# Local attention heads beside the token products, and the first units of w_out_2 by halves of the tokens between the other heads

## The reference, cut to what matters

```
def second_block(x, positions, norm_g, w_in, swa_sink, ..., w_out, final_norm):
    for l in range(DEPTH_2):
        h = rmsnorm_2(x, norm_g[l])
        proj = jnp.einsum('bsd,de->bse', h, w_in[l])
        (a_q, a_k, a_v, a_g, b_cq, b_ckv, b_kr, b_g,
         c_q, c_k, c_v, c_g) = jnp.split(proj, SPLIT_OFFSETS, axis=-1)
        ya = swa_attention(...)     # 8 local heads of 128, 2 key heads, a sink
        yb = mla_attention(...)     # 4 heads, queries, keys and values from latents
        yc = diff_attention(...)    # 4 pairs of heads of 64, then a norm
        y = jnp.concatenate([ya * jax.nn.silu(a_g), yb * jax.nn.silu(b_g),
                             yc * jax.nn.silu(c_g)], axis=-1)
        x = x + jnp.einsum('bse,ed->bsd', y, w_out[l])
    return rmsnorm_2(x, final_norm)
```

## Time and profile before

| | |
|---|---|
| median of 3 runs | 2373.35 us |
| span of the profiled execution | 2372.3 us |
| TensorE busy | 2273.5 us, 96% |
| VectorE busy | 1363.0 us, 57% |
| ScalarE busy | 1055.6 us, 44% |
| mean granted TensorE clock | 0.978 |

### The profile page before, as it was taken

How to read it: one execution, slowest core, us unless ns; L and a number is a source line. 1 busy time by engine, 2 the same in 40 slices (tenths; PEclk the granted TensorE clock), 3 DMA queues, 4 the chain that set the end, 5 groups by cost and what they waited for, 6 DMA issues and landing times.

```text
span 2372.3 us, 31751 instructions
## 1 busy us (share of the span) xinstructions
PE 2273.5 (96%) x13038; PEld 1973.5 (83%) x13038; DVE 1363.0 (57%) x1694; ACT 1055.6 (44%) x1366; POOL 57.7 (2%) x66
## 2 busy tenths in 40 slices
PE   8999989899989999999999999999998999999898
PEld 7888978787877888888888887888976889898676
DVE  5545656475566666766766444644456454444654
ACT  5433443423455545454555333533445443343543
POOL 0000020011000000000000000000000000000000
PEclk9999998899999999999999999999999999999999
DMA  8556520013634555555565556555531556564033
GB/s 282 193 168 221 178 88 1 1 32 139 202 127 137 190 183 193 179 193 183 189 205 187 194 195 197 195 185 183 170 99 36 178 176 221 162 202 161 1 125 141
DMA packets 235977, 373.07 MB, mean 157 GB/s; under 512 B 8359, under 2 KB 108244, under 8 KB 235092
## 3 DMA queue, kind: packets, MB, share of 16 engines
q1 hardware_dynamic: 229740, 362.89, 46.3%
q10 hardware_dynamic: 6120, 8.50, 1.0%
HBM read 369.25 MB, written 2.12 MB: 157 GB/s over the span
## 4 chain that ended last, share of the span: by engine, by line
PE 64%; DVE 5%; issue 5%; ACT 2%; POOL 0%; DVEq 0%; POOLq 0%; ACTq 0%
PE PS L465 16%; PE PS L424 12%; PE PS L426 12%; PE PS L425 12%; PE PS L468 8%; PE PS L1941 1%; PE PS L1925 1%; DVE w_lo L342 1%; ACT w_hi L337 1%; DVE small L1979 1%; DVE spare L1975 1%; PE PS L904 1%; ACT spare L1953 0%; DVE h_both L921 0%; PE PS L2608 0%
## 5 line engine op out<-in xcount | busy, mean ns | idle before, releaser
L342 DVE TENSOR_TENSOR w_lo<-raw,w_hi 128x2048 fp32r<-128x2048 f32 (+2 forms) x340 | 766.4, 2254 | 766.5 <-ACT w_hi L337 766.2
L337 ACT ACTIVATE w_hi<-raw 128x2048 fp32r<-128x2048 f32 (+2 forms) x340 | 641.2, 1886 | 842.4 <-PE PS L426 487.4
L465 PE MATMUL PS<-h_both,w_hi 128*128 128x512 f32 x1968 | 539.4, 395 | 2.9 <-DVE h_both L921 1.8
L424 PE MATMUL PS<-w_hi,h_both 128*128 128x512 f32 (+2 forms) x1344 | 511.6, 381 | 11.3 <-DVE h_both L921 4.6
L425 PE MATMUL PS<-w_lo,h_both 128*128 128x512 f32 (+2 forms) x1344 | 508.3, 378 | 0.0
L426 PE MATMUL PS<-w_hi,h_both 128*128 128x512 f32 (+2 forms) x1088 | 408.7, 376 | 0.0
L465 PEld LDWEIGHTS PS<-h_both,w_hi 128*128 128x128 f32 x1968 | 336.6, 189 | 49.5 <-DVE h_both L921 2.8
L468 PEld LDWEIGHTS PS<-h_both,w_lo 128*128 128x128 f32 x1968 | 302.1, 189 | 42.1
L468 PE MATMUL PS<-h_both,w_lo 128*128 128x256 f32 x1968 | 313.1, 281 | 0.0
L424 PEld LDWEIGHTS PS<-w_hi,h_both 128*128 128x128 f32 x1344 | 255.3, 190 | 59.8 <-DVE h_both L921 5.1
L425 PEld LDWEIGHTS PS<-w_lo,h_both 128*128 128x128 f32 x1344 | 255.1, 190 | 45.8
(11 more groups left out here) (508 smaller groups left out, 2027.1 us busy)
## 6 DMA issues: line engine op xcount, KB each, us to landing
raw<-in_w_in SPq DMA_DIRECT2D x132, 1024.0 KB, 5.2
raw<-in_ffn_w_up SPq DMA_DIRECT2D x176, 512.0 KB, 4.4
raw<-in_w_out SPq DMA_DIRECT2D x48, 1024.0 KB, 5.1
raw<-in_ffn_w_down SPq DMA_DIRECT2D x44, 1024.0 KB, 5.1
raw<-in_mem_wkv SPq DMA_DIRECT2D x8, 1024.0 KB, 11.6
raw<-in_mem_wq SPq DMA_DIRECT2D x4, 1024.0 KB, 5.3
raw<-in_mem_wo SPq DMA_DIRECT2D x4, 1024.0 KB, 7.0
raw<-in_w_in SPq DMA_DIRECT2D x4, 768.0 KB, 4.7
```

The costliest lines, as they stand in the source:

```text
L337: act.activation(w_hi[:, slot % 2, :st.n], raw[:, slot, :st.n], ACT.Copy).then_inc(hi_made, 1)
L342: dve.tensor_tensor(w_lo[:, slot % 2, :st.n], raw[:, slot, :st.n], w_hi[:, slot % 2, :st.n].bitcast(F32), ALU.subtract).then_inc(lo_made, 1)
L424: pe.matmul(ps, l_hi, r_hi, start=start, stop=False, skip_group_check=skip)
L465: pe.matmul(sums, wh[:, k, cs], h_both[:, :, kk, :], start=kk == 0, stop=False, skip_group_check=True)
```

## The change

- The eight local heads leave the head stage. They run on four lanes of their own (banks 4 to 7) as `fill` between the units of tok and tok_end, one step after each unit, with more rounds between a head's steps. Their lane n starts n + 1 units in. The Silus of their gates move with them (`local_gates_scalar`).
- The head stage keeps 8 diff heads on four lanes (two rounds), the latents and 4 MLA heads (the latter idle for 9 to 11 rounds).
- Their working room moves from `spare` (where the slots of `w_hi` and `w_lo` lie) to other places, so that one of the two split slots can be filled during the stage. The diff heads' squares go to the lane's own room, with one wait on ScalarE for it.
- Unit 0 of w_out_2 is split before the last evacuation of c_vg. Units 0, 1 and 2 are each multiplied in two halves, first the upper 128 tokens, then the lower (`multiply_rows`), at set rounds between the heads. Turns 0 to 3 (the local heads' rows) use bank 7. Unit 3 stays whole.
- The waits at the start of the stage (latents, gates, small loads) stay; semaphores that nothing used are left out.

```
+        def multiply_rows(pe, q, j, t, ready=None):
+            st, bank, slot = q.st, 2 * q.parity + t, (q.first + j) % 2
+            if j == 0 and t == 0:
+                pe.wait_ge(act_evac, q.number(-1))
+                pe.wait_ge(dve_evac, q.number(-1))
+            pe.wait_ge(lo_made, q.unit(j + 1))
+            if ready:
+                ready()
...
+            for k in range(st.kb):
+                kk = j * st.kb + k
+                last = three_pass(pe, PS[:, bank, :st.n_cols], h_hi[:, kk, t * P:(t + 1) * P], h_lo[:, kk, t * P:(t + 1) * P],
+                                  wh[:, k, :], wl[:, k, :], kk == 0, kk == st.units * st.kb - 1)
+            if t == TB - 1:
+                last.then_inc(unit_used, 1)
...
+                if job["h"] == 1:
+                    turns = t_mixed[job["layer"]]
+                    pe.wait_ge(turns.dve, turns["lo3"])
+                elif job["h"] > 1:
+                    diff_made(pe, job["layer"])
...
+        def local_tensor(pe, j):
...
+            (q, k), = job["pairs"]
+            for t_ in range(TB):
+                last = pe.matmul(PS[:, bank, t_ * S:(t_ + 1) * S], q[:, t_ * P:(t_ + 1) * P], k, start=True, stop=True)
+            last.then_inc(j.pe, 1)
+            yield
+            yield
+            yield
+            pe.wait_ge(j.act, j["exp1"])
...
+            last.then_inc(j.pe, 1)
+            yield
+            yield
+            pe.wait_ge(j.act, j["copied"])
...
+            last.then_inc(j.pe, 1)
+            yield
+            yield
...
+        def beside_products(part, e, layer):
+
+            made = L2[layer]["local"]
+            return together(*[one_by_one([rounds(n + 1)] + [part(e, j) for j in js]) for n, js in enumerate(made)])
...
+        def local_gates_scalar(act, layer):
+            g, st = L2[layer]["gates"], ST2[layer]["tok"]
+            for n in range(2):
+                yield from rounds(6 if n == 0 else 4)
+                act.wait_ge(act_evac, st.G + n + 1)
+                act.wait_ge(dve_evac, st.G + n + 1)
+                g_ = ztok[:, :, AG + 512 * n:AG + 512 * (n + 1)]
+                act.activation(g_, g_, ACT.Silu).then_inc(g.act, 1)
...
-            jobs = [latents] + swa + diff + mla
-            for job in jobs:
+            jobs = [latents] + diff + mla
+            for job in swa + jobs:
                 job["layer"] = layer
-            for job in mla[1:]:
-                job["idle"] = 3
-            L2[layer].update(latents=latents, swa=swa, diff_heads=diff)
-            SWA, DIFF_, MLA = 1, 9, 17
-            picks = [[SWA + 6, DIFF_ + 0, DIFF_ + 4], [SWA + 7, DIFF_ + 1, DIFF_ + 5], [0, MLA], [SWA, SWA + 1, MLA + 1],
-                     [DIFF_ + 2, DIFF_ + 6], [DIFF_ + 3, DIFF_ + 7], [SWA + 2, SWA + 3, MLA + 2],
-                     [SWA + 4, SWA + 5, MLA + 3]]
-            return on_lanes(jobs, picks, starts)
+            for job, idle in zip(mla[1:], (9, 11, 11)):
+                job["idle"] = idle
+            L2[layer].update(latents=latents, diff_heads=diff,
+                             local=on_lanes(swa, [[n, 4 + n] for n in range(4)], local_starts, local_lanes))
+            DIFF_, MLA = 1, 9
+            for n in (2, 3):
+                diff[n]["idle"] = 1
+            picks = [[DIFF_ + n, DIFF_ + 4 + n] for n in range(4)] + [[0, MLA], [MLA + 1], [MLA + 2], [MLA + 3]]
+            return on_lanes(jobs, picks, starts, late_lanes)
...
-        MIXED_ROUND = 15
+        MIXED_BANKS = (7, 7, 7, 7, 4, 5, 6, 5)
...
         def mixed_tensor(pe, layer, j):
-            for _ in range(MIXED_ROUND):
-                yield
-            free_lanes_made(pe, layer)
-            for n in (0, 1):
+            q, d = Group(ST2[layer]["out"], 0), L2[layer]["diff"]
+            yield
+            local_made(pe, layer)
+            for n in range(4):
                 mixed_turn(pe, j, n)
-            yield
-            yield
-            for n in (2, 3):
+                if n == 2:
+                    multiply_rows(pe, q, 0, 0, ready=lambda: pe.wait_ge(j.dve, j["lo1"]))
+                yield
+                if n == 2:
+                    multiply_rows(pe, q, 0, 1)
+                yield
+            multiply_rows(pe, q, 1, 0, ready=lambda: pe.wait_ge(j.dve, j["lo3"]))
+            yield
+            yield
+            yield
+            multiply_rows(pe, q, 1, 1)
+            yield
+            pe.wait_ge(d.dve, d["n11"])
+            for n in (4, 5):
                 mixed_turn(pe, j, n)
             yield
+            yield
+            for made in lanes2[layer][4:6]:
+                pe.wait_ge(made[-1].dve, made[-1].dve1)
+            mixed_turn(pe, j, 6)
+            multiply_rows(pe, q, 2, 0, ready=lambda: pe.wait_ge(j.dve, j["lo5"]))
+            yield
 
         def mixed_scalar(act, layer, j):
-            for _ in range(MIXED_ROUND):
-                yield
-            free_lanes_made(act, layer)
-            split_hi(act, Group(ST2[layer]["out"], 0), 0)
-            yield
-            for n in (0, 1):
+            q = Group(ST2[layer]["out"], 0)
+            yield
+            yield
+            for n in range(4):
                 mixed_hi(act, j, n)
-            yield
-            for n in (2, 3):
+                yield
+                if n == 0:
+                    split_hi(act, q, 1)
+                if n == 3:
+                    split_hi(act, q, 2)
+                yield
+            yield from rounds(4)
+            for n in (4, 5):
                 mixed_hi(act, j, n)
+            split_hi(act, q, 3)
+            yield
+            yield
+            mixed_hi(act, j, 6)
             yield
 
         def mixed_vector(dve, layer, j):
-            for _ in range(MIXED_ROUND):
-                yield
-            ssq, d = L2[layer]["ssq"], L2[layer]["diff"]
+            q, ssq, d = Group(ST2[layer]["out"], 0), L2[layer]["ssq"], L2[layer]["diff"]
+            yield
+            yield
+            for n in range(4):
+                mixed_lo(dve, j, n)
+                yield
+                if n == 0:
+                    split_lo(dve, q, 1)
+                if n == 3:
+                    split_lo(dve, q, 2)
+                yield
+            yield
             for job in L2[layer]["diff_heads"]:
                 dve.wait_ge(job["steps"].act, job["steps"].act1)
             dve.tensor_scalar(ssq, ssq, 1.0 / P, EPS, ALU.mult, ALU.add).then_inc(d.dve, 1)
             yield
-            split_lo(dve, Group(ST2[layer]["out"], 0), 0)
-            yield
-            for n in (0, 1):
-                mixed_lo(dve, j, n)
-            yield
-            for n in (2, 3):
-                mixed_lo(dve, j, n)
-            yield
-
-        def mixed_opening_tensor(pe, layer, j):
-            st, d = ST2[layer]["out"], L2[layer]["diff"]
-            multiply(pe, Group(st, 0), 0, ready=lambda: pe.wait_ge(j.dve, j["lo1"]))
-            yield
-            lanes_made(pe, lanes2[layer])
-            pe.wait_ge(d.dve, d["n11"])
-            for n in (4, 5):
-                mixed_turn(pe, j, n)
-            multiply(pe, Group(st, 0), 1, ready=lambda: pe.wait_ge(j.dve, j["lo3"]))
-            yield
-            for n in (6, 7):
-                mixed_turn(pe, j, n)
-            multiply(pe, Group(st, 0), 2, ready=lambda: pe.wait_ge(j.dve, j["lo5"]))
-            yield
-            multiply(pe, Group(st, 0), 3, ready=lambda: pe.wait_ge(j.dve, j["lo7"]))
-            yield
-
-        def mixed_opening_scalar(act, layer, j):
-            q = Group(ST2[layer]["out"], 0)
-            lanes_made(act, lanes2[layer])
-            split_hi(act, q, 1)
-            yield
-            for n in (4, 5):
-                mixed_hi(act, j, n)
-            yield
-            split_hi(act, q, 2)
-            for n in (6, 7):
-                mixed_hi(act, j, n)
-            yield
-            split_hi(act, q, 3)
-            yield
-
-        def mixed_opening_vector(dve, layer, j):
-            q = Group(ST2[layer]["out"], 0)
-            lanes_made(dve, lanes2[layer])
-            split_lo(dve, q, 1)
             run(diff_rows(dve, layer))
+            yield
             yield
             for n in (4, 5):
                 mixed_lo(dve, j, n)
-            yield
-            split_lo(dve, q, 2)
-            for n in (6, 7):
-                mixed_lo(dve, j, n)
-            yield
             split_lo(dve, q, 3)
+            yield
+            yield
+            mixed_lo(dve, j, 6)
+            yield
+
+        def mixed_opening_tensor(pe, layer, j):
+            q = Group(ST2[layer]["out"], 0)
+            lanes_made(pe, lanes2[layer])
+            mixed_turn(pe, j, 7)
+            multiply_rows(pe, q, 2, 1)
+            multiply(pe, q, 3, ready=lambda: pe.wait_ge(j.dve, j["lo7"]))
+            yield
...
-                for name in ("kv", "tok", "tok_end"):
-                    run(products_tensor(pe, st[name]))
+                run(products_tensor(pe, st["kv"]))
+                fill = beside_products(local_tensor, pe, layer)
```

(9 more changed lines are left out.)

190 lines of the change are left out of this document (131 added, 59 removed).

## The result

| | before | after |
|---|---|---|
| median of 4 runs | 2373.36 us (2368.74 to 2374.34) | 2356.7 us (2356.39 to 2357.76) |
| span of the profiled execution | 2372.3 us | 2354.7 us |
| mean granted TensorE clock | 0.978 | 0.982 |

The ratio is 0.9937, 95% interval 0.9923 to 0.9951: the change saves 16.7 us by the medians and 17.6 by the two profiled executions. The forecast was 2356.4, the range 2346 to 2367.

What follows compares the result with a forecast made beforehand. TensorE, busy 96% of the span, loses time only by waiting or running slowly. Per layer 68.0 work, 7.7 waits, 1.7 clock, 18.2 local heads, 1.0 interruptions: 96.6; gains 8.1 and 8.8, together 16.9, give 2356.4 us (2346 to 2367).

Steps and rivals of the forecast that it cites:

- Local heads among the token products: Token products: the heads' 18.2 us per layer move, interruptions add 0.06 each, 1.0 in all; other engines priced at nothing.
- The round with a Silu: ScalarE's densest round in the token products: result ready after 11.6 us, TensorE comes after about 13.9, 2.3 us left.
- Unit 0 split early: Before the last token evacuation: both engines split while TensorE multiplies the last unit, 5.5 us against 1.9 + 2.3; nothing late.
- (a): Start of the stage: TensorE waits 0.9 us for the last evacuation, as before.
- (b): Fifth diff score: TensorE waits 3.0 us for lane 0's puts, behind a VectorE split, then 0.4 for lane 1.
- (c): Seventh diff score: TensorE waits 1.4 us for lane 2's puts, behind a v copy, biases and maxima, then 0.4.
- (d): Last mixed turn: TensorE waits 1.6 us, as VectorE's split of unit 3 stands before the last two puts.
- One half-clock stretch of 1.7 per layer: After the 3 us wait for lane 0's puts: 1.7 us lost once per layer; bounds none and twice 1.7.
- The sum of 96.6: Per layer, token-product end to fourth w_out_2 unit plus moved local heads and interruptions: 96.6 us after, against 104.7 and 105.4.
- Rival 1: Stage waits mostly covered, no half clock follows, interruptions free: 25 us gained in all, 2348; chance 0.2.
- Rival 2: VectorE bounds the short stage: diff-score waits double, second half-clock stretch, about 1.6 us gained per layer, 2370; chance 0.12.
- Rivals 3 and 4: Token products: interruptions dear, at 1.0 us each 2386, chance 0.04; local heads don't fit, splits late, 2387, chance 0.01.

Runs made afterwards that it cites:

- after_again: The changed kernel unmodified, run again as the reference beside three follow-up kernels: median 2350.76 us (2349.37 to 2356.36, 5 runs).
- whole_units: Against the changed kernel, units 0 to 2 of w_out_2 multiplied whole after the last turn, splits of 2 and 3 behind the heads: 2374.85 us.
- late_unit0: Against the changed kernel, both engines split unit 0 of w_out_2 in the stage, right before unit 1: 2363.36 us (2359.54 to 2364.16, 5 runs).

## Why the prediction was right, point by point

- **TensorE's waits in the stage are the lever, its work is not.** Right. TensorE's work is the same (its instructions are the same in number), and 16.2 of the 17.6 us stand between the first matmul of kv and the fourth w_out_2 unit of the two layers. The token products grew by 18.2 where the text had 19.
- **Local heads among the token products: 18.2 moved, 1.0 for 16 interruptions, none of it late.** Measured 18.2 together, so the 1.0 was too much. The interruption was 0.06 in the text and is 0.02 or less by the experiment, and by the rows of one unit less than nothing. The other engines had the room: there is no wait of TensorE in the token products but the 1.8 us one behind them that both kernels have. What the text left out is that the clock can fall behind that wait: in the profiled execution of before it did so in layer 1 alone, in that of after in both, 1.5 us.
- **The round with a Silu has 2.3 us left.** Right by its outcome: the table load is 1283 ns, as in the earlier trace rows, in all five places of the stretch, and no wait follows a Silu. By the Trainium skill's 2.7 us for every change of table set (ScalarE: Activation LUTs, Rules for kernel authors) each of these rounds would have been 0.5 us late; the trace disagrees with that figure. From the end of a split (1613.85) to the start of the Silu behind its table load (1615.17) are 1.32 us.

```profile
L2086 ACT ACT_TABLE_LOAD x3 | 3.8, 1283 | 0.1
...
L2505 ACT ACT_TABLE_LOAD x2 | 2.6, 1283 | 0.0
```

- **Unit 0 split early: nothing is late.** Right, and shown by its reverse. From c_qk to the stage, where the split was added, the stretch without half clock takes 94.37 us before and 94.39 in after_again.
- **(a) 0.9.** As before, 0.89.
- **(b) 3.0 and 0.4.** Measured 2.71 and 1.0. The chain was right in each link, and everything came some tenths later than put. In us from the start of the stage, and each step on VectorE taken as over when the next one starts, the split on ScalarE was put at 14.9 to 16.8 and ran from 15.2 to 17.1, VectorE's split was to end at 19.1 and ended at 19.4, the v copy 19.7 and 20.1, the low part 20.4 and 20.7, the puts 21.0 and 21.2. TensorE was put there at 18.0 and came at 18.6. These are the rows of VectorE:

```profile
1786.36 2.29 DVE L343 TENSOR_TENSOR w_lo<-raw,w_hi 128x2048 fp32r<-128x2048 f32 x1 [3.17 <-ACT w_hi L338]
...
1788.71 0.67 DVE L2777 COPY arena<-PS 128x512 f32<-128x512 f32 x1
1789.30 0.68 DVE L2833 TENSOR_TENSOR h_both<-PS,h_both 128x512 fp32r<-128x512 f32 x1
1789.89 0.60 DVE L2664 TENSOR_SCALAR arena<-PS,small 128x128 f32<-128x128 f32 x2
```

What the walk did not see is that the chain has a second arm of nearly the same length, TensorE's own v product, copy and low part. It makes no difference to the sum, and all of it to what an improvement brings.
- **(c) 1.4 and 0.4.** Measured 1.13 and 0.9.
- **(d) 1.6.** Measured 1.20, and caused by the split, as said.
- **One half-clock stretch of 1.7 per layer.** Right as a mean, not as a rule: behind the same 2.71 us wait the kernel after lost 0 in layer 0 and 1.7 in layer 1, and 3.4 and 1.7 in the other profiled execution.
- **The sum of 96.6.** Measured 77.15 + 18.2 = 95.35 and 78.8 + 18.2 = 97.0. Several misses cancel in it. The visible waits are 5.9 and the pauses of the two second lanes 1.9, together 7.8, where the text had 7.7. TensorE's own work is 77.15 - 7.8 = 69.3 in layer 0 and not 68.0: it is put together in smaller pieces, a half unit takes 12 matmuls of 0.227 and about 0.1 more, and each wait has the tail of a group before it. Against these 1.3 stand the 1.0 for interruptions, which cost nothing, and in layer 0 the 1.7 of half clock that did not come: 96.6 + 0.1 + 1.3 - 1.0 - 1.7 = 95.3. In layer 1 it came.
- **The stage of 77 to 78 us.** Measured 77.15 and 78.8.
- **The time of 2356.4.** Measured 2356.7, and that it is so near is luck. Apart from the misses that cancel, the same kernel took 2350.76 in its other five runs, with the same waits in the stage of the profiled one. That is just below the forecast's own range of 2351 to 2362 and within the stated one.
- **Rival 1**, mostly covered waits: no, the visible waits are those of the forecast; its free interruptions came true. **Rival 2**, VectorE as the bound: not in this kernel, it is busy for 43.7 of 77 us; but the kernel with whole units is this rival's case in all but name, with waits for VectorE and a longer time at half clock, at 2374.85. **Rivals 3 and 4**: excluded.

Where did the gain come from, then? A good part of it is the clock. Without the half-clock loss the stretch took 104.7 - 5.1 = 99.6 and 105.4 - 5.1 = 100.3 us before, and 95.35 and 95.3 after (the local heads' 18.2 counted in): 9.3 us from waits. The loss in the stage itself fell from 10.2 to 1.7 us in these executions, which is 8.5, and behind the 1.8 us wait ahead of it 1.5 us of that were lost again. In the other profiled execution of the kernel after the loss in the stages was 5.1, and none behind that wait. The prediction had both terms but never set them apart. (Part of the slow stretch of before lay inside its waits, where it cost nothing, so the split between the two is rough.)

## What to carry to other kernels

Where TensorE waits for steps of other engines in a short stage, moving part of the stage away shortens nothing unless other TensorE work is put into the gaps: heads moved alone gave 0, heads moved with half units between the others gave 17 to 20 us. Look then for long instructions (here a split of 2.3 us) that stand on another engine's queue in front of short ones that TensorE waits for, and move them to where TensorE is full; follow every arm that ends at the wait, since removing one may only uncover the next (0.8 + 2.8 us apart, 5.4 together). Where single runs differ by more than the effect, compare the same stretch in two traces, best of all in executions where the clock did not fall in it; and take both ends of the stretch inside the changed part, since what lies ahead of it moves its start as well.

## What the runs showed of the hardware that was not expected

- **The loss to the half clock comes in equal portions.** Summed in steps of 2 us it was 0, 1.7, 3.4, 5.1 or 6.8 us in each of the stages looked at. One in layer 1 of the kernel after, behind the 2.71 us wait there:

```profile
2222.00:2224.00 2.00, 2.00 (x11) 1.61 (x11) 0.00 (x0) 0.13 (x2) 0.00 (x0) 0.83 0.77 292
2224.00:2226.00 2.00, 2.00 (x12) 2.00 (x11) 0.00 (x0) 0.00 (x0) 0.00 (x0) 0.50 0.00 0
2226.00:2228.00 2.00, 2.00 (x5) 0.81 (x5) 0.00 (x0) 0.00 (x0) 0.00 (x0) 0.82 0.00 0
```

  0.50 is 1.2 of 2.4 GHz. Behind the same wait in layer 0 the clock stayed at 1.00. Behind the single waits of 0.9 to 1.2 us in the stages of the table it never fell, behind one of 3.9 (whole_units) or 4.91 (late_unit0) it fell in both layers, and between them it did so in some cases and not in others: at 1.90 in one layer of the two, at 2.11 in neither, at 2.71 in seven of ten. The 1.81 us wait in front of c_qk stands in both layers of all eleven traces, and the clock fell behind it in 16 of these 22 cases. One portion costs 1.5 us there: from c_qk to the stage it is 94.4 us without it and 95.8 or 95.9 with it. What decides it is open. The row behind that wait in layer 0 of the kernel after:

```profile
1674.00:1676.00 2.00, 2.00 (x11) 2.00 (x11) 2.00 (x2) 0.48 (x2) 0.00 (x0) 0.50 0.79 200
```
- **Executions of one kernel differ by where these portions fall.** The two profiled executions of the kernel after are 7.1 us apart (spans 2354.7 and 2347.6), with the same waits in the stages. The difference was there before the first of them: the stage of layer 0 began at 1769.21 in one and at 1761.27 in the other, and kv at 1532.38 and 1525.90. Up to 1500 us the half-clock loss was 34.2 us in one and 25.6 in the other. The table of stretches from 200 to 400 us, first of the slower, then of the faster, has the clock at 0.94 against 0.97 (from 400 to 600 us 0.94 against 0.96):

```profile
200.00:400.00 200.00, 191.25 (x1280) 172.91 (x1278) 126.79 (x201) 78.47 (x112) 17.05 (x18) 0.94 0.37 120
```
```profile
200.00:400.00 200.00, 190.48 (x1296) 171.79 (x1295) 128.00 (x205) 79.75 (x116) 17.07 (x18) 0.97 0.37 120
```

- **Changing between float32 products and products of split weights costs TensorE next to nothing**: 0.02 us or less a time, by the 16 interruptions of a layer.
